# More unread products in the waits of a two-network kernel: attention tail, scan, gate chain, router, second attention

## The reference

```python
def first_block(...):
    h = concatenate([meta, x], 1)
    for i in range(2):
        mix = diff_attention(...) if i % 2 == 0 else rwkv7_time_mix(...)
        ...                       # layer_norm(ALPHA * h + mix), then FFN or experts, then layer_norm

def rwkv7_time_mix(...):
    ...
    _, y_fwd = lax.scan(_wkv7_step, S0, ...)
    _, y_bwd = lax.scan(_wkv7_step, S0, ..., reverse=True)
    y = y_fwd + y_bwd
    y = (y - mean(y)) * rsqrt(var(y) + RW_LNX_EPS) * lnx_g + lnx_b     # per head
    bonus = sum(rh * kdh * r_k) * v
    return ((y + bonus) * g) @ w_o

def moe_swiglu(...):
    probs = softmax(x @ w_router + b_router)
    top_p, top_i = top_k(probs, 2)
    gates = sum(one_hot(top_i) * top_p / sum(top_p))
    for e in range(8):
        y = y + gates[..., e:e + 1] * swiglu(x, w_gate[e], w_up[e], w_down[e])
    return y
```

## Time and profile before

| what | value |
|---|---|
| median of 3 runs | 2710.91 us (2710.58 to 2719.76) |
| profiled execution | 2723.02 us |
| its span | 2721.2 us |
| mean granted clock of TensorE | 0.971 |
| TensorE busy | 2559.6 us, 94% |
| VectorE busy | 1993.2 us, 73% |
| ScalarE busy | 1526.0 us, 56% |
| records of fills (L435) | 74 |

### The profile page before, as it was taken

One profiled execution on the slowest core, in us unless ns is written; L12 is line 12 of the kernel. 1 busy time (PEld: TensorE's weight loads), 2 busy tenths in 40 slices (PEclk: granted clock), 3 DMA queues, 4 the chain that ended last, 5 costly groups with the idle time before them and its releaser, 6 DMA issues. The chain is left out here.

```text
span 2721.2 us, 47747 instructions
## 1 busy us (share of the span) xinstructions
PE 2559.6 (94%) x20277; PEld 2108.3 (77%) x20277; DVE 1993.2 (73%) x2855; ACT 1526.0 (56%) x2207; POOL 181.3 (7%) x192
## 2 busy tenths in 40 slices
PE   8999999989997999999999999998999889999888
PEld 7779987689964676767676676666969879969778
DVE  7855549555357999999898999895857865757865
ACT  5634434323124777878787787764446454446444
POOL 0000000020002800000000000100200101200101
PEclk9999999999988999999999999999989999999999
DMA  6315533400033999999999999974515534625533
GB/s 195 101 62 186 163 132 115 136 20 4 4 138 140 384 365 377 366 378 374 374 378 366 378 377 367 360 300 130 175 54 173 178 118 140 195 62 171 169 106 104
DMA packets 264614, 565.87 MB, mean 208 GB/s; under 512 B 25996, under 2 KB 204356, under 8 KB 221260
## 3 DMA queue, kind: packets, MB, share of 16 engines
q1 hardware_dynamic: 257580, 547.02, 57.1%
q0 software_dynamic: 5248, 10.23, 1.2%
q10 hardware_dynamic: 1568, 5.51, 0.6%
HBM read 545.41 MB, written 11.53 MB: 205 GB/s over the span
## 5 line engine op out<-in xcount | busy, mean ns | idle before, releaser
L319 DVE TENSOR_TENSOR wl<-raw,wh 128x1024 fp32r<-128x1024 f32 (+1 forms) x610 | 742.8, 1224 | 337.4 <-ACT wh L310 321.7
L310 ACT ACTIVATE wh<-raw 128x1024 fp32r<-128x1024 f32 (+1 forms) x610 | 639.9, 1053 | 459.6 <-PE PS L163 404.6
L319 DVE TENSOR_TENSOR wl<-early,wh 128x1024 fp32r<-128x1024 f32 x384 | 466.5, 1228 | 52.8 <-ACT wh L310 33.9
L310 ACT ACTIVATE wh<-early 128x1024 fp32r<-128x1024 f32 x384 | 405.9, 1060 | 130.9 <-PE PS L163 115.0
L161 PE MATMUL PS<-wh,xe_h 128*96 128x512 f32 x896 | 357.5, 399 | 10.6 <-DVE wl L319 8.8
L161 PE MATMUL PS<-b_hn_h,wh 128*128 128x256 f32 (+1 forms) x1152 | 339.6, 295 | 21.1 <-DVE wl L319 14.6
L162 PE MATMUL PS<-wl,xe_h 128*96 128x512 f32 x896 | 354.3, 395 | 0.0
L163 PE MATMUL PS<-wh,xe_l 128*96 128x512 f32 x896 | 354.2, 395 | 0.0
L162 PE MATMUL PS<-b_hn_l,wh 128*128 128x256 f32 (+1 forms) x1152 | 332.2, 288 | 0.0
L163 PE MATMUL PS<-b_hn_h,wl 128*128 128x256 f32 (+1 forms) x1152 | 331.9, 288 | 0.0
L161 PEld LDWEIGHTS PS<-b_hn_h,wh 128*128 128x128 f32 (+1 forms) x1152 | 225.7, 196 | 27.5 <-DVE wl L319 16.9
(11 more groups left out here) (495 smaller groups left out, 4952.3 us busy)
## 6 DMA issues: line engine op xcount, KB each, us to landing
early<-in_moe_in SPq DMA_DIRECT2D x128, 1024.0 KB, 6.8
raw<-in_moe_in SPq DMA_DIRECT2D x96, 1024.0 KB, 6.7
raw<-in_w_in SPq DMA_DIRECT2D x76, 1024.0 KB, 5.4
early<-in_moe_out SPq DMA_DIRECT2D x64, 1024.0 KB, 5.9
raw<-in_moe_out SPq DMA_DIRECT2D x48, 1024.0 KB, 5.2
raw<-in_attn_w_in SPq DMA_DIRECT2D x24, 512.0 KB, 5.2
raw<-in_rw_w_rkv SPq DMA_DIRECT2D x12, 1024.0 KB, 5.1
raw<-in_ffn_w_gate SPq DMA_DIRECT2D x11, 1024.0 KB, 5.3
```

The costliest lines, as they stand in the source:

```text
L310: act.e.activation(st.two(n)[0], st.raw(n), ACT.Copy).then_inc(*act.sig("hi", st.name, n, sem=f"hi_{st.name}"))
L319: dve.e.tensor_tensor(lo, st.raw(n), hi.bitcast(F32), SUB).then_inc(*dve.sig("lo", st.name, n, sem=f"lo_{st.name}"))
```

## The change

`busy_pe` is called with larger counts and at new places: 134 calls of the matmul in place of 37, thus 268 records for 74. The places:

- norms 1 and 3: 12 in place of 5;
- `turned(n)` for items 19 to 23: 8, 4, 4, 3, 2, in bank 4, behind the wait for bank 2 and ahead of the wait for `diff`;
- `back(w)` for the three waves: 4 each, ahead of the wait for "xu"; `upd(0)`: 4, ahead of its waits;
- "y": 5 in place of 3; behind `spread(0)` and `spread(1)`: 3 each;
- router: 4 ("count"), 3 ("rank"), 3 ("rows") and 12 ("picks"), each in the bank that the next user takes, so that this user waits for the fill;
- `third(0)` of each layer of the second network: 8, in bank 2.

VectorE gets one more wait, for the second constants ("c_b2") ahead of the causal add.

```diff
--- before.py
+++ after.py
@@ -451,7 +451,7 @@
             pe.wait_ge(pe.at("ln_sq", key, k // 2))
             t = pe.e.matmul(PS[:, b, 0:Tn], ones, LNQ[:, k, 0:Tn], start=k == 0, stop=k == KC - 1)
         t.then_inc(*pe.sig("ln_mm", key, "var"))
-        busy_pe(pe, 5, key)
+        busy_pe(pe, 12 if key % 2 else 5, key)
 
     def norm_act(act, key, hi=None, st=None):
 
@@ -535,6 +535,7 @@
     at_xs = two("at_x", KC, T)
     at_u = [tile(f"at_u{n}", T) for n in range(2)]
     ITEMS = [(h, i) for h in range(8) for i in range(3)]
+    TAIL = {19: 8, 20: 4, 21: 4, 22: 3, 23: 2}
 
     def attention_order(unit, v_turned, scores, turned, values, sums):
 
@@ -595,6 +596,8 @@
             b, before = bank("turned", n, b=2)
             if before:
                 pe.wait_ge(pe.at(*before))
+            if n in TAIL:
+                busy_pe(pe, TAIL[n], "tail", n, at=4)
             pe.wait_ge(pe.at("diff", n))
             for kt, (k0, kn) in enumerate(QT):
                 t = e.transpose(PS[0:kn, b, kt * 128:kt * 128 + qn], at_c[n % NP_][0:qn, k0:k0 + kn], ident[0:qn, 0:qn])
@@ -1101,6 +1104,7 @@
             for i in range(BL):
                 x = e.transpose(PS[:, 4 + i // 4, i % 4 * 128:i % 4 * 128 + n], PAD[0:n, i * 128:(i + 1) * 128], ident[0:n, 0:n])
             x.then_inc(*pe.sig("scan_mm", "back", w))
+            busy_pe(pe, 4, "back", w, at=turn[0] % 4)
             for g in gs:
                 pe.wait_ge(pe.at("xu", g))
             for b in range(4):
@@ -1173,6 +1177,8 @@
             x.then_inc(*pe.sig("scan_mm", "res", g))
 
         def upd(g):
+            if g == 0:
+                busy_pe(pe, 4, "upd", at=turn[0] % 8)
             pe.wait_ge(pe.at("res", g))
             pe.wait_ge(pe.at("inverse", g))
             b = take("upd", g)
@@ -1245,7 +1251,7 @@
         pe.wait_ge(pe.at("raw", "A", m))
         gate(0)
         gate(1)
-        busy_pe(pe, 3, "y", at=1)
+        busy_pe(pe, 5, "y", at=1)
         pe.wait_ge(pe.at("y_var_r"))
         first_units = project_units(pe, SA, "rw_o", [("rw_o", i) for i in range(4)], po_y, T, ("x_lo", "rw_o"),
                                     (4, 5, 6, 7))
@@ -1254,6 +1260,8 @@
                 spread(take("y_norm", f, b=f % 2), f).then_inc(*pe.sig("y_norm_mm", f))
             if f >= 2:
                 next(first_units, None)
+            if f < 2:
+                busy_pe(pe, 3, "spread", f, at=7 - f)
             if f + 2 < KC:
                 gate(f + 2)
             if f + 2 == KC:
@@ -1766,12 +1774,14 @@
                     for j, (p0, pn) in enumerate(QT):
                         t = e.transpose(PS[0:pn, b, j * NE:(j + 1) * NE], gt[0:NE, p0:p0 + pn], ident[0:NE, 0:NE])
                     t.then_inc(*pe.sig("logits_mm"))
+        busy_pe(pe, 4, "count", at=turn[0] % 8)
         b, before = bank("count")
         pe.wait_ge(pe.at(*before))
         for i, (q0, qn) in enumerate(QT):
             pe.wait_ge(pe.at("mk", i))
             t = e.matmul(PS[:, b, 0:8], ones[0:qn, :], mk[i][0:qn], start=i == 0, stop=i == 2)
         t.then_inc(*pe.sig("count_mm"))
+        busy_pe(pe, 3, "rank", at=turn[0] % 8)
         pe.wait_ge(pe.at("c_moe"))
         for i, (q0, qn) in enumerate(QT):
             b, before = bank("rank", i)
@@ -1781,12 +1791,14 @@
                 t = e.matmul(PS[0:qn, b, 0:8], tri[0:jn, 0:qn] if j == i else ones[0:jn, 0:qn], mk[j][0:jn], start=j == 0,
                              stop=j == i)
             t.then_inc(*pe.sig("rank_mm", i))
+        busy_pe(pe, 3, "rows", at=turn[0] % 8)
         for i, (q0, qn) in enumerate(QT):
             for x, src in enumerate((rk[i], sc[i][:, 56:64])):
                 b, before = bank("rows", i, x)
                 pe.wait_ge(pe.at(*before))
                 pe.wait_ge(pe.at("gate", i) if x else pe.at("rank", i))
                 e.transpose(PS[0:NE, b, 0:qn], src[0:qn], ident[0:qn, 0:qn]).then_inc(*pe.sig("rows_mm", i, x))
+        busy_pe(pe, 12, "picks", at=turn[0] % 8)
         at_branch = turn[0], dict(holder)
 
         def sparse(pe):
@@ -2607,6 +2619,8 @@
 
         def third(n):
             h, i = ITEMS2[n]
+            if n == 0:
+                busy_pe(pe, 8, "b_shares", l, at=2)
             b, before = bank("b_turned", l, n, b=2)
             pe.wait_ge(pe.at(*before))
             pe.wait_ge(pe.at("b_shares", l, n))
@@ -2925,6 +2939,7 @@
             if p == 2 or p == 20:
                 i = p // 20
                 o, ca = score[:, i, 0:128 * (i + 1)], causal[:, i, 0:128 * (i + 1)]
+                dve.wait_ge(dve.at("c_b2"))
                 dve.wait_ge(dve.at("scored", l, i, 15))
                 e.tensor_tensor(o, o, ca, ADD).then_inc(*dve.own())
             elif p in (11, 29):
```

## The result

The changed kernel is slower: 2734.88 us, median of 3 runs (2733.16 to 2737.79), against 2710.91 before. The ratio is 1.0064, 95% interval 1.004 to 1.0088, thus +17 us (11 to 24); the two medians themselves lie 24 us apart, with three runs each. The forecast was 2724, with 2706 to 2741 as the range. The profiled executions differ by less: 2733.16 us after, 2723.02 before, +10.1. Before's profiled execution was slow for its kind: in later comparisons 35, 29 and 26 runs of the kernel before had medians of 2719.3, 2716.2 and 2717.7. So +10 is what the two traces have to explain, and the common difference is nearer to 20.

A forecast was written before the change was run, and what follows sets the result against it. It took TensorE, busy 94% of the span at nearly full clock, as the bound. Terms 4.7 + 0.7 + 6.6 - 5.5 + 7.2 - 0.4 = +13.3 us gave 2736.3 profiled, 2724.2 as median; range 2706 to 2741.

The forecast's parts named there:

- main case: Whole kernel: each fill costs its length less idle time and faster work behind; +13.3 us, range 2716 to 2733, chance 0.58.
- rival 2: Router decides: flag's load and branch come behind "picks", upd(0)'s fill runs cold, tail at upper bound; +25, 2736; chance 0.19.
- attention's tail: Attention's tail, +21 calls: later fills in series with ScalarE's copies, L628 +6.4 late, 1.7 back; +4.7 us.
- norms 1 and 3: Norms 1 and 3, +14 calls: fills outlast the gaps, less faster work behind them; +0.7 us.
- scan: Scan, +16 calls at three back waves and upd(0): fills exceed gaps or wait on VectorE; +6.6 us.
- chain behind the scan: Chain behind the scan, +8 calls: steps of 6.23 us fall to about 3.5 at full clock; -5.5 us.
- router: Router, +22 calls: fills stand behind waits and "picks" delays L1892, so the first expert starts later; +7.2 us.
- second network's items: Second network's first items, +16 calls: 6.9 us fills in 5.46 us gaps, against cold products behind; -0.4 us.
- rival 3: Slow stretches the change does not touch shrink too; 10 to 15 us more come back, about 2711; chance 0.13.
- Fill less gap: At every fill: it costs what it is longer than the idle time it lies in; 0.86 us per call at full clock.
- `upd(0)`: In the scan: the fill itself waits on VectorE and runs mostly cold, 1.55 comes back; +3.7 us.
- The branch: Router, TensorE's flag load and branch behind "picks": bounded by 0 and 3.56 us, taken as 0, done while fills are queued.

The follow-up runs named there:

- all again: The whole changed kernel timed once more in five rounds against the kernel before: ratio 1.0084, +23 us.
- tail: The kernel before with only the fills of the attention's tail added (8, 4, 4, 3, 2): ratio 1.0021 to the kernel before, +5.7 us.
- The last pair of runs: Kernel before plus the attention tail's fills and 8 more calls, one ahead of each narrow product or all ahead of the first: 1.0048 and 1.0031 to before.

## Why the prediction was right

The forecast of 2724 lay 11 us below the median and its range held it. The main case's own range, 2716 to 2733, did not: the median lies beside the 2736 of rival 2, whose mechanism did not happen. So the mechanism of the main case was right and its size too small, by 4 us in the first comparison and by 10 in the second. Term by term, in the profiled executions, forecast and measured:

```
term                     forecast   after   all again
attention's tail            +4.7     +7.4      +5.6
norms 1 and 3               +0.7     +0.2      +0.2
scan                        +6.6     +5.9      +8.8
chain behind the scan       -5.5     -5.0      -5.0
router                      +7.2     +6.5      +8.0
second network's items      -0.4      0         0
stages without an edit       0       -4.9      -4.9
sum                        +13.3    +10.1     +12.7
```

The nearness of the sums is in part luck. The rows of the places with fills add to +15.0 and +17.6 in the two traces, and stages without an edit, to which the forecast gave nothing, took 4.9 off; that is rival 3 in kind, with less than half of its size. The row on the norms is read at norm 1 alone; norm 3 takes 0.2 off again in both traces.

- **Fill less gap.** The starts that the sum gave for the tail were 133.3, 138, 142.1 and 145 for the transposes of items 20 to 23, and 154.4 for L631; they came at 133.2, 139.6, 143.3, 146.1 and 153.8. In the router VectorE's P and the first product with it were to be 5.0 and 8.7 late: 16.3 less the 11.6 that had come from ahead is 4.7, and 19.8 less 11.6 is 8.2.
- **The wrong step: "Its followers ran at the lower level for some 3.4 us, so half of that, 1.7, comes back."** Nothing came back. The clock fell all the same, behind fills that had kept it full from 119 to 156 us: for 6.8 us in "after" and in "tail", and for 3.4, as before, in "all again". The last pair of runs shows the reason at this place: the eight narrow products, not idle time. The term was 4.7 and measured 5.6 to 8.3.
- **`upd(0)`.** The bank's wait was read rightly off the order. I took the fill as mostly slow after that wait; at 612.28 it ran at full clock, 3.70 us, and 1.6 of the followers' time came back: +2.0 for 3.7. The scan's sum came out near the forecast, or above it, all the same, because `back(0)` and the products behind it cost 2.8 and 5.2 in place of 1.4; the pauses at L1120 are part of that.
- **The branch** was done under the fill, as the sum had it: 0.15 us ahead of L1904. Rival 2 fell by its own mark, since L1892's successor at 872.2 is 860.6 with the 11.6 taken off. By the Trainium skill's page "Advanced Engine Details and Errata", section "Engine Queue Depths", TensorE's queue holds 64; the 24 records of "picks" and an immediate start behind them agree with that.
- **The rule on the clock.** The Trainium skill's page "TensorE: Matmul & The Clock Gate", section "Terms", puts the penalty at the throttled time times (1 - K/N), where K/N is the share of the clock that is granted, 0.5 here. The slow time fell by 82 us, which by this would give 41 us back. The prediction's objection was that much of the slow time is waiting. That is so in the router (8.6 of 13.7 us idle), but not in the kernel: TensorE was busy in 127 of the 158 slow us before, and in 65 of the 76 after. Half of the 62 us that went is 31, close to the 29.3 by which the work other than fills became shorter. So this gain was real, and it was smaller than the price: against the fills' added 85.4 us TensorE's idle time fell by only 46.0.
- **The median.** I carried +13.3 over from the profiled execution. The runs gave +17 and, repeated, +23. Before's profiled execution, 2723.0, was 4 to 7 us slower than the medians of the three larger sets of runs, and the changed kernel's were not slow for their kind (2733.2 and, repeated, 2735.7 with a median of 2738.0). So an ordinary execution of before had less slow time to give back, and the granted clocks of the timed runs bear this out: of the 90 of before, the 20 with 0.971, as in the profiled one, took 2720.8 on average, the 34 with 0.973 took 2718.0, and the 10 with 0.975 took 2714.6. Where it has it less is open: no second trace of before was taken.

## What to carry to other kernels

A filler costs its own length less the idle time that is ahead of it, so put it ahead of the wait, count it from that row (here gap / 0.86 us), and check in the changed order what its bank waits for: a filler that stands behind the wait adds all of itself and runs slow. Count the slow time in which TensorE works, where a faster clock is time, place by place (here 19 of 20.5 us in the chain, 5 of 13.7 in the router), and set it against the fill that it takes. Undo a tuned set of fillers site by site: of four sites timed alone, three cost, and the gain of the one that was to pay is not clear of the noise; fitted counts, without `upd(0)`, "rank", "rows" and four of the tail's five fills, took 0.3% off the time in place of adding 0.6 to 0.8%.

## What the runs showed of the hardware

- The granted clock fell from full to 0.53 with TensorE 7.00 of 7 us busy (156 to 163 us), and to 0.50 with it 3.00 of 3 busy after 10.5 us of unbroken fill. One wide product ahead of each narrow one (8 rows) kept it at 1.00.
- In stages without any edit slow stretches of a few us came and went between executions, and moved a stage by -3.5 to +4.9 us. A single profile can't tell a gain of a few us at the end of the program; the shift at the place itself can.
- After a fill of 12 calls the flag's load and branch on TensorE cost nothing, where VectorE stood 3.51 us ahead of P.
